# A four-mixer decoder step on one core: in passes 2 and 3 the mLSTM projection goes ahead of the output projection as filler of the HGRN mixer

## What is computed

```python
h = rmsnorm(x, norm_w[l])
proj = h @ w_in[l]                       # 1024 -> 3592 columns, cut among four mixers
s5  : complex diagonal state space model, then GELU and a sigmoid gate
hg  : HGRN2, chunked gated recurrence with a decay per channel
ml  : mLSTM, chunked, with a running maximum (log_i, log_f per head) and a normaliser
rt  : retention, chunked, with rotary embedding
mixed = concat(s5 * silu(g), hg * silu(g), ml * silu(g), rt * silu(g))
x = x + mixed @ w_out[l]
```

## Time and profile before

| | |
|---|---|
| median of 3 runs | 1749.5 us (1747.79 to 1751.62) |
| the profiled execution | 1754.27 us |
| its span, first to last instruction | 1752.5 us |
| busy: PE, DVE, ACT, POOL | 1501.6, 855.3, 518.3, 391.9 us |
| mean granted TensorE clock | 0.877 of full speed |

### The profile page before, as it was taken

How to read it: one execution, slowest core, us unless ns; L and a number is a source line. 1 busy time by engine, 2 the same in 40 slices (tenths; PEclk the granted TensorE clock), 3 DMA queues, 4 the chain that set the end, 5 groups by cost and what they waited for, 6 DMA issues and landing times. The chain is left out here.

```text
span 1752.5 us, 29173 instructions
## 1 busy us (share of the span) xinstructions
PE 1501.6 (86%) x11415; PEld 1319.5 (75%) x11415; DVE 855.3 (49%) x2555; ACT 518.3 (30%) x1053; POOL 391.9 (22%) x398
## 2 busy tenths in 40 slices
PE   1867899889779999889889989989999998897695
PEld 1756788689668988787777878868888888786383
DVE  6756654542883336447244445455265527433322
ACT  3435422332333322123223333233243412210101
POOL 3312233321002322232000333332102323120000
PEclk9988999879889989887699999987999989795697
DMA  5222133232244240273213412323225232071254
GB/s 155 86 79 56 50 98 121 82 97 76 67 134 111 74 99 25 40 173 90 60 58 104 127 60 88 121 81 97 82 70 151 63 82 53 27 131 55 66 181 147
DMA packets 181567, 158.33 MB, mean 90 GB/s; under 512 B 72944, under 2 KB 169784, under 8 KB 179640
## 3 DMA queue, kind: packets, MB, share of 16 engines
q1 hardware_dynamic: 108632, 82.94, 17.6%
q10 hardware_dynamic: 72800, 73.54, 14.3%
HBM read 128.68 MB, written 27.76 MB: 89 GB/s over the span
## 5 line engine op out<-in xcount | busy, mean ns | idle before, releaser
L973 POOL TENSOR_TENSOR wlo<-wraw,whi 128x512 fp32r<-128x512 f32 (+1 forms) x224 | 292.8, 1337 | 516.1 <-ACT whi L1016 516.1
L2066 PE MATMUL psum<-whi,hhi 128*128 128x256 f32 (+1 forms) x1008 | 311.1, 309 | 14.4 <-DVE r L1383 4.8
L2066 PE MATMUL psum<-wlo,hhi 128*128 128x256 f32 (+1 forms) x1008 | 300.2, 298 | 0.0
L2066 PE MATMUL psum<-whi,hlo 128*128 128x256 f32 (+1 forms) x1008 | 300.0, 298 | 0.0
L2350 PE MATMUL psum<-wraw,mixT 128*128 128x256 f32 (+1 forms) x1152 | 263.7, 389 | 13.8 <-DVE r L1392 6.7
L2350 PEld LDWEIGHTS psum<-wraw,mixT 128*128 128x128 f32 (+1 forms) x1152 | 211.1, 186 | 58.7 <-DVE small L1740 11.8
L2061 PE MATMUL psum<-hhi,whi 128*128 128x288 f32 (+2 forms) x672 | 231.7, 345 | 3.1 <-DVE hlo L1431 1.6
L2066 PEld LDWEIGHTS psum<-whi,hhi 128*128 128x128 f32 x1008 | 208.6, 207 | 25.1 <-issue 20.7
L2061 PE MATMUL psum<-hhi,wlo 128*128 128x288 f32 (+2 forms) x672 | 221.7, 330 | 0.0
L2061 PE MATMUL psum<-hlo,whi 128*128 128x288 f32 (+2 forms) x672 | 221.5, 330 | 0.0
L2066 PEld LDWEIGHTS psum<-wlo,hhi 128*128 128x128 f32 x1008 | 208.8, 207 | 0.7 <-issue 0.5
(11 more groups left out here) (306 smaller groups left out, 2253.2 us busy)
## 6 DMA issues: line engine op xcount, KB each, us to landing
wraw<-in_w_in ACTq DMA_DIRECT2D x50, 1024.0 KB, 5.4
wraw<-in_w_out ACTq DMA_DIRECT2D x16, 1024.0 KB, 5.5
x<-xo SPq DMA_DIRECT2D x64, 128.0 KB, 2.2
r<-x SPq DMA_DIRECT2D x16, 512.0 KB, 4.4
r<-in_c_rot SPq DMA_DIRECT2D x4, 1088.0 KB, 7.0
wraw<-in_w_in ACTq DMA_DIRECT2D x4, 1056.0 KB, 5.5
r<-in_x_prompt SPq DMA_DIRECT2D x8, 512.0 KB, 4.9
r<-WTm SPq DMA_DIRECT2D x4, 1024.0 KB, 11.9
```

The costliest lines, as they stand in the source:

```text
L973: nc.gpsimd.tensor_tensor(wlo[:, hslot[b], ks, 0:width], wraw[:, wslot[b], ks, 0:width], whi[:, hslot[b], ks, 0:width].bitcast(F32), ALU.s ...
L2066: mm = nc.tensor.matmul(bank.t[:, 0:width], x[:, kt, c], w[:, sl, kt, 0:width], start=first, stop=last)
```

## The change

In passes 0 and 1 nothing is different. In passes 2 and 3 the filler of the HGRN mixer is the mLSTM projection with `mlpre` first and the output projection of pass n-1 second.

```diff
     for n in passes:
-        plan += weave(head, filler + project(n, "ml", {"ml_ifg": [(("mlpre", n), None)]}))
+        ml = project(n, "ml", {"ml_ifg": [(("mlpre", n), None)]})
+        plan += weave(head, filler + ml if n < 2 else ml + filler)
         plan += [(("mlpre", n), "store")] if "ml" in parts else []
```

## The result

The median rose from 1750.6 to 1810.0 us (four runs each); the ratio of after to before is 1.0333 [1.0279, 1.0387]. The forecast was 1795, with a range of 1762 to 1817. The profiled execution of after took 1807.6 us (span 1805.8) against 1754.3 before, 53.3 more.

What follows compares the result with a forecast made beforehand. Both touched stretches were taken as PE's time plus PE's waits. Pass 2 +15.3, pass 3 +27.4 and clock +3 sum to 45.7 us, which on the median of 1749.5 gives 1795, range 1762 to 1817.

Steps and rivals of the forecast that it cites:

- the clock: Both passes: stretches at the lower clock around three more waits over 4 us cost +3 us (0 to 9).
- (n): mLSTM mixer of pass 3: rs comes late behind the `rt_v` load and POOL's split, with no slack, +3.8 us.
- (f): mLSTM mixer of pass 2: rs comes late behind the `rt_v` load and POOL's split, +1.5 us (0 to 3.6).
- (i): Pass 3, C(0): PE is there after two pieces and waits for `hg_st`, +1.9 us.
- (k): Pass 3, piece k00: mlpre ahead of A0(2) on DVE makes the take of q01 late, +10.4 us.
- (c): Pass 2, mlpre: PE waits for the take of ifg3, queued behind Q(0), +8.3 us.
- (d): Pass 2, piece v1: waits for the take of k0, with a table load for Exp behind Ln, +2 us.
- (a): S5 stage ahead of pass 2: the `ml_ifg` split delays Square and slows DVE's products, +2.5 us (1.1 to 4.4).
- (g): S5 stage ahead of pass 3: the `ml_ifg` split delays Square and slows DVE, +4.2 us (2.2 to 5.5).
- overlap (1772): Rival, passes 2 and 3: waits overlap instead of adding, 24 us instead of 46, 1772; chance 0.22.
- "POOL's splits hit harder" (1812): Rival, passes 2 and 3: POOL's splits meet A0 or A1 on DVE, 13 to 17 us more, 1812; chance 0.14.
- Faster: Rival, passes 2 and 3: ACT reaches the takes in time, only gains of 12.5 us stay, 1737; chance 0.07.

Runs made afterwards that it cites:

- pass2_only: After's new order in pass 2 alone, with pass 3 keeping the order of before; ratio to before 1.0126 [1.0100, 1.0152].
- small_split_after: After, with GpSimd splitting only 8 columns of each mLSTM weight block in passes 2 and 3; ratio to before 1.0316 [1.0289, 1.0342].
- before_pre_k: Before, with the mLSTM preparation of passes 2 and 3 put behind the k pieces instead of the gates; ratio to before 0.9969 [0.9953, 0.9986].
- small_split_before: Before, with GpSimd splitting only 8 columns of each mLSTM weight block in passes 2 and 3; ratio to before 0.9976 [0.9958, 0.9994].

## Why the prediction was right, and where its terms were not

The direction, the mechanism and most waits came as forecast. The sum was 45.7 on the profiled execution, measured 53.3. That the sum came so near is in part luck: the clock and (n) were together 12 us too low, and (f), (i) and (k) 5 us too high.

- (b) 6.81 for 6.6; (c) 7.90 for 8.3, with no wait before the second chunk and the 5.00 gone; (e) 2.17 for 2.1; (j) 4.97 for 4.9; (l) 4.43 for 4.8. These are pure queue arithmetic, and they held.
- (k) 8.39 for 10.4: right in kind, 2 too large. The take came when forecast, 24.6 us behind m for 24.3; PE was there 2.4 late, as the piece behind the preparation took 5.40 us for 3.3.
- (d) 4.19 for 2: the upper end of its bounds, since POOL's split did meet the third chunk. (h) +1.6 for +1.1. (m) waits of 1.00, 1.26 and 1.35 are gone, 3.6 for 2.5.
- (i) 0.30 for 1.9: the pieces ahead of it took 8.23 us instead of 6.1, so that the wait had turned into slow work.
- (a) VectorE's chain is 2.4 longer for the 2.5 forecast, but all of it by the split; Square's 1.1 didn't show. The total doesn't show (a): PE is at the end of that stage within 0.5 us of before, and the wait for `yd` just ahead differs by more than the term from run to run. (g) 5.3 by the parts, for 4.2; B grew by 5.9.
- (f) in pass 2: a wait of 2.25 that is made up again, so nothing instead of 1.5 (pass2_only).
- (n) is the mis-sized term: D grew by 8.6 instead of 3.8, of it 7.0 idle. I took 5.45 us for the load from a row where the queues were quiet, and followed the moved step on ACT and POOL but not on SyncE's queue, whose loads the last output pieces pushed onto it.
- The clock is the other: 10.6 us of additional busy time in the two stretches, for 3 (0 to 9), so above its own bounds. Windows of after, columns as above:

```profile
919.70:930.00 10.30, 10.01 (x134) 8.79 (x134) 3.77 (x12) 1.99 (x8) 0.10 (x1) 0.84 0.01 2
1276.60:1285.00 8.40, 8.38 (x50) 8.16 (x51) 0.62 (x2) 0.35 (x1) 0.00 (x0) 0.72 0.01 2
1310.70:1319.00 8.30, 8.23 (x48) 8.02 (x48) 4.74 (x16) 5.98 (x11) 0.11 (x1) 0.71 0.01 2
1329.50:1337.00 7.50, 7.41 (x36) 6.38 (x37) 0.40 (x1) 5.36 (x10) 3.06 (x3) 0.57 0.01 2
```

Each of these stretches stands behind a wait of 3 to 7 us and runs partly at 1.2 GHz instead of 2.4: the granted clock is 0.57 to 0.84, and a piece costs up to 2.4 us more (5.46 instead of 3.10 behind the 8.39 wait, 4.61 instead of 3.10 behind the 6.81 wait). I had charged it for three waits; it comes behind nearly all. No run separates it from the waits.

Of the rivals, overlap (1772) fell: no wait was shortened by another but (i) and part of (k), and there the clock took it. "POOL's splits hit harder" (1812) has the right total (1810) for a wrong reason: small_split_after gives back only 3 us. Faster fell at its own point: the take of the last gate piece came 7.9 us after PE wanted it.

## What to carry to other kernels

A long chain of small steps on a shared engine belongs behind the last urgent work in that engine's queue, not as early as its inputs allow: moved behind the last chunk, the same preparation gave back about 10 us a pass in after and 7 in pass 2 of before, and no wait over 1.5 us followed it there within A and C. When a filler is swapped for another, count what it wants from the engines that serve it (an add of 0.4 us for an output piece, a take on ACT behind 8 us of chunk work for a projection piece), and follow every queue that the moved steps block, SyncE's included. Confirm small terms by the length of a chain or a stretch, not by one wait that another chain can also set.

## What the runs showed of the hardware

- A load of 1 MB of weights took 6.8 us with the queues nearly quiet, 9.9 beside a table of 1.1 MB, 13.3 beside the table and eight state loads, four of them of 2 KB in single elements, which SyncE needed 7.9 us to issue (5.5 in before).
- The wait of VectorE for the same read of `yd` (544 KB) was 3.57 us in before, 6.90 in before_pre_k and 7.23 in small_split_before, with no difference in order up to there. It moves a wait of PE by as much.
- What a wait costs is more than its length: 27.7 us of additional idle in the two stretches came with 10.6 us of additional busy time, for the same matmuls at a granted clock of 0.93 for 0.97 and 0.90 for 0.95.
